# A reordered seam ahead of the first feed-forward: turning X before its row factors are known

## The reference

```python
o = jnp.concatenate([o_mla, o_gla], axis=-1) @ w_out[l]
x = x + gate_m * rms_norm(o, g_post_mix[l])

h = rms_norm(x, g_pre_ffn[l]) * (1.0 + scale_f) + shift_f
f = (jax.nn.silu(h @ w_ffn_gate[l]) * (h @ w_ffn_up[l])) @ w_ffn_down[l]
x = x + gate_f * rms_norm(f, g_post_ffn[l])
```

## Time and profile before

| | |
|---|---|
| median of 3 runs | 2699.1 us (2698.87 to 2699.74) |
| profiled execution, whole | 2705.51 us |
| its span | 2703.7 us |
| mean granted TensorE clock | 0.981 |

### The profile page before, as it was taken

The page is one execution under the profiler, slowest core; times in us unless marked ns, Lnnn a source line. Parts: engine busy times, 40 slices in busy tenths (PEclk is TensorE's granted clock), DMA queues, the critical chain, the costliest instruction groups (busy, mean ns, idle before and its releaser), DMA issues.

```text
span 2703.7 us, 30651 instructions
## 1 busy us (share of the span) xinstructions
PE 2602.7 (96%) x12149; PEld 2158.3 (80%) x12149; DVE 1668.6 (62%) x1700; ACT 1151.0 (43%) x1217; POOL 0.2 (0%) x4
## 2 busy tenths in 40 slices
PE   5899999899999999999999999999899999999998
PEld 4778778788887888887988888787688888888886
DVE  7878788856665555557446665655555555555556
ACT  5244544443333333335445455444653333333333
POOL 0000000000000000000000000000000000000000
PEclk8999999899999999999999999999999999999999
DMA  9979969977776555554854444554455555555553
GB/s 330 360 262 324 330 220 324 243 252 253 254 253 209 190 192 191 186 186 157 239 172 140 150 147 152 171 202 153 143 187 186 186 189 191 193 188 186 186 187 139
DMA packets 268139, 568.20 MB, mean 210 GB/s; under 512 B 9857, under 2 KB 46591, under 8 KB 258704
## 3 DMA queue, kind: packets, MB, share of 16 engines
q1 hardware_dynamic: 265986, 563.83, 61.9%
q10 hardware_dynamic: 2064, 3.15, 1.0%
HBM read 561.69 MB, written 5.24 MB: 210 GB/s over the span
## 4 chain that ended last, share of the span: by engine, by line
PE 80%; DVE 5%; ACT 3%; issue 2%; DMA 1%; DVEq 0%; ACTq 0%
PE bank L1283 25%; PE bank L1285 24%; PE bank L1284 24%; ACT wh L631 2%; DVE wl L1964 1%; DVE ROWB L1964 1%; DVE ACC L1985 1%; DMA raw<-in_w_out 1%; PE bank L1252 1%; PE bank L1816 1%; PE bank L1645 1%; PE bank L1764 1%; PE bank L1799 0%; DVE X L2118 0%; DMA raw<-in_w_uq 0%
## 5 line engine op out<-in xcount | busy, mean ns | idle before, releaser
L1964 DVE TENSOR_TENSOR wl<-raw,wh 128x2048 fp32r<-128x2048 f32 (+4 forms) x434 | 975.6, 2248 | 875.6 <-ACT wh L631 875.1
L631 ACT ACTIVATE wh<-raw 128x2048 fp32r<-128x2048 f32 (+4 forms) x434 | 816.4, 1881 | 1317.9 <-PE bank L1285 1209.8
L1283 PE MATMUL bank<-wh,XTh 128*128 128x512 f32 (+4 forms) x2680 | 1044.5, 390 | 21.9 <-DVE wl L1964 15.9
L1285 PE MATMUL bank<-wh,XTl 128*128 128x512 f32 (+4 forms) x2680 | 1032.5, 385 | 0.0
L1284 PE MATMUL bank<-wl,XTh 128*128 128x512 f32 (+4 forms) x2680 | 1031.6, 385 | 0.0
L1283 PEld LDWEIGHTS bank<-wh,XTh 128*128 128x128 f32 x2680 | 506.1, 189 | 126.8 <-issue 18.3
L1285 PEld LDWEIGHTS bank<-wh,XTl 128*128 128x128 f32 x2680 | 505.5, 189 | 94.4
L1284 PEld LDWEIGHTS bank<-wl,XTh 128*128 128x128 f32 x2680 | 506.2, 189 | 91.1 <-issue 0.5
L1283 PE MATMUL bank<-wh,HTh 128*128 128x512 f32 x640 | 251.1, 392 | 3.0 <-DVE ROWB L1964 3.0
L1285 PE MATMUL bank<-wh,HTl 128*128 128x512 f32 x640 | 249.2, 389 | 0.0
L1284 PE MATMUL bank<-wl,HTh 128*128 128x512 f32 x640 | 249.1, 389 | 0.0
(11 more groups left out here) (317 smaller groups left out, 1502.8 us busy)
## 6 DMA issues: line engine op xcount, KB each, us to landing
raw<-in_w_ada SPq DMA_DIRECT2D x96, 1024.0 KB, 6.3
raw<-in_w_in SPq DMA_DIRECT2D x48, 1024.0 KB, 5.2
raw<-in_w_ffn_gate SPq DMA_DIRECT2D x44, 1024.0 KB, 5.2
raw<-in_w_ffn_up SPq DMA_DIRECT2D x44, 1024.0 KB, 5.2
raw<-in_w_ffn_down SPq DMA_DIRECT2D x44, 1024.0 KB, 5.0
raw<-in_w_gate SPq DMA_DIRECT2D x44, 1024.0 KB, 5.2
raw<-in_w_up SPq DMA_DIRECT2D x44, 1024.0 KB, 5.1
raw<-in_w_down SPq DMA_DIRECT2D x44, 1024.0 KB, 5.0
```

The lines of the kernel that those rows point to most:

```text
L631: act.activation(wh[:, st.lin % 2, 0:width], raw[:, st.raw % 4, 0:width], ACT.Copy).then_inc(hi_made, 1)
L1283: pe.matmul(out_, hi_t[:, k, rows], w[0][:, q, :], start=first and q == 0, stop=False)
L1285: mm = pe.matmul(out_, lo_t[:, k, rows], w[0][:, q, :], start=False, stop=last and q == n - 1)
L1964: return dve.tensor_tensor(out_, a, b, op)
```

## The change

X is turned as it is, without the factor 1/rms of its rows, as soon as the pieces of X are added. The row factors, which lie one to a partition, have to be laid along the free dimension to be applied behind the turn: VectorE puts them on a diagonal (`DIAG` = identity times factor), TensorE multiplies a matrix of ones by it, and ScalarE copies the result to `WIDE_INV`. VectorE multiplies the turned groups by it on their way from PSUM to `FTMP`. Groups 0 and 1 go row block by row block, so that the first gate slab can start with row block 0; gain and shift are applied there by VectorE, and for groups 2 to 7 by ScalarE, which writes the high part and the float32 value with one activation each. `slab_mm` gets a hook `row_ready`. ScalarE's `hi()` for gate slab 1 goes ahead of the squares, which become four of 1024 columns; `chunk_left("o")` and the issue of the write of `rel_scratch` go behind the high parts of row block 1. Cut to its core:

```diff
...
-TURNS = [("mem", 8, 2), ("x", 8, 1), ("cq", 2, 2), ("ckv", 1, 2), ("o", 8, 0), ("f1", 8, 1), ("z2", 8, 2),
+TURNS = [("mem", 8, 2), ("x", 8, 1), ("cq", 2, 2), ("ckv", 1, 2), ("o", 8, 0), ("f1", 10, 0), ("z2", 8, 2),
...
+        FTMP = at("FTMP", [P, 4, 512], zb + 4 * 4096)
+        DIAG = at("DIAG", [P, RB, P], zb + 4 * 10240)
+        WIDE_INV = at("WIDE_INV", [P, SEQ], zb + 4 * 10496)
...
-            chunk_left("o")
-            act.wait_ge(S("rel_row"), 2)
-            act.dma_start(rel_d, relrow[:, :].unsqueeze(1).broadcast_to([NH, P, REL_W])).then_inc(S("rel_out"), 16)
+            hi()
+
+            def f1_wide(r):
+
+                act.wait_ge(S("turned"), TURN0["f1"] + 3 * r + 3)
+                f(WIDE_INV[:, P * r:P * r + P], PB[2][:, P * r:P * r + P], ACT.Copy, "f_wide")
+
+            def f1_row_hi(r, b):
+
+                act.wait_ge(S("f_made"), 2 * r + b + 1)
+                rows = slice(P * r, P * r + P)
+                f(XTh[:, 2 * b:2 * b + 2, rows], FTMP[:, b, :].rearrange("p (t n) -> p t n", t=2)[:, :, rows], ACT.Copy, "turn_hi")
+
+            def f1_group_hi(b):
+
+                act.wait_ge(S("gained"), TURN_N["x"] + 3 + b)
+                for kt in (2 * b, 2 * b + 1):
+                    half = slice(SEQ * (kt % 2), SEQ * (kt % 2) + SEQ)
+                    src = FTMP[:, b % 4, half]
+                    kw = dict(scale=modA[:, 3, kt:kt + 1], bias=modA[:, 2, kt:kt + 1])
+                    act.activation(XTh[:, kt, :], src, ACT.Identity, **kw)
+                    ins = act.activation(src, src, ACT.Identity, **kw)
+                ins.then_inc(S("turn_hi"), 1)
 
             def ffn(k, pre, after, more, gain=None):
 
                 if k == 0:
                     j = NORMS.index(pre)
                     for r in range(RB):
-                        for c in range(4):
-                            act.wait_ge(S("x_added"), 4 * r + c + 1)
-                            if c + r:
-                                act.wait_ge(S("x_sq"), 4 * r + c)
-                            f(JUNK2[:, 512 * c:512 * c + 512], X[:, r, 512 * c:512 * c + 512], ACT.Square, "x_sq",
+                        for c in range(2):
+                            if (r, c) == (1, 1):
+                                f1_wide(0)
+                            act.wait_ge(S("x_added"), 4 * r + 2 * c + 2)
+                            if r:
+                                act.wait_ge(S("x_sq"), c + 1)
+                            f(JUNK2[:, 1024 * c:1024 * c + 1024], X[:, r, 1024 * c:1024 * c + 1024], ACT.Square, "x_sq",
                               accum_out=xsq[:, r, c:c + 1])
-                            if (r, c) in ((1, 0), (1, 3)):
-                                act.wait_ge(S("squared"), RB * j + r + (c == 3))
-                                part = slice(0, 1) if c == 0 else slice(1, 2)
-                                f(nstat[:, j, 1, part], nstat[:, j, 0, part], ACT.Sqrt, "row_rooted" if c == 0 else "rooted",
-                                  scale=1.0 / D, bias=eps[:, 0:1])
-                turn_hi(pre, XTh, gain=gain, between=hi)
+                        if r:
+                            f1_row_hi(0, 0)
+                        act.wait_ge(S("squared"), RB * j + r + 1)
+                        f(nstat[:, j, 1, r:r + 1], nstat[:, j, 0, r:r + 1], ACT.Sqrt, "rooted" if r else "row_rooted", scale=1.0 / D,
+                          bias=eps[:, 0:1])
+                    f1_row_hi(0, 1)
+                    f1_wide(1)
+                    f1_row_hi(1, 0)
+                    f1_row_hi(1, 1)
+                    chunk_left("o")
+                    act.wait_ge(S("rel_row"), 2)
+                    act.dma_start(rel_d, relrow[:, :].unsqueeze(1).broadcast_to([NH, P, REL_W])).then_inc(S("rel_out"), 16)
+                    act.wait_ge(S("mod_ready"), 10)
+                    for b in range(2, 8):
+                        f1_group_hi(b)
+                        if b in (3, 5):
+                            hi()
+                else:
+                    turn_hi(pre, XTh, gain=gain, between=hi)
...
-                    if name == "f1":
-                        pe.wait_ge(S("normed"), RB * 3 + 1 + b // 2 + 1)
...
-            def slab_mm(banks, kts, width, first, last, lhs=None, row_done=None, row_free=None):
+            def slab_mm(banks, kts, width, first, last, lhs=None, row_done=None, row_free=None, row_ready=None):
 
...
+                    if row_ready is not None:
+                        row_ready(r)
...
+            def f1_turn(b, rows=range(RB)):
+
+                for k in range(2):
+                    for r in rows:
+                        mm = pe.transpose(PB[4 + b % 4][:, SEQ * k + P * r:SEQ * k + P * r + P],
+                                          X[:, r, P * (2 * b + k):P * (2 * b + k) + P], ident)
+                return mm
+
+            def f1_rows(r):
+
+                pe.wait_ge(S("turn_free"), TURN0["f1"] + 2 * r + 2)
+
...
-                            rows = X if k else ROWB
-                            turn_into(pre, lambda r, q: rows[:, r, P * q:P * q + P],
-                                      lambda: None,
-                                      lambda s: slab_mm((0, 1), ALL[4 * s:4 * s + 4], 512, s == 0, s == 3), "xo" if k else None)
+                            first_slab = lambda s: slab_mm((0, 1), ALL[4 * s:4 * s + 4], 512, s == 0, s == 3,
+                                                           row_ready=f1_rows if k == 0 and s == 0 else None)
+                            if k:
+                                turn_into(pre, lambda r, q: X[:, r, P * q:P * q + P], lambda: None, first_slab, "xo")
+                                return
+                            for r, b in ((0, 0), (0, 1), (0, 2), (1, 0), (1, 1), (0, 3), (1, 2), (1, 3)):
+                                pe.wait_ge(S("x_added"), 4 * r + b // 2 + 1)
+                                if b == 3:
+                                    pe.wait_ge(S("mod_ready"), 10)
+                                f1_turn(b, (r,))
+                            for r in range(RB):
+                                pe.wait_ge(S("normed"), RB * 3 + r + 1)
+                                pe.matmul(PB[2][:, P * r:P * r + P], ones, DIAG[:, r, :], start=True, stop=True)\
+                                    .then_inc(S("turned"), 3)
+                            first_slab(0)
+                            f1_turn(4).then_inc(S("turned"), 1)
+                            f1_turn(5).then_inc(S("turned"), 1)
+                            pe.wait_ge(S("turn_free"), TURN0["f1"] + 6)
+                            first_slab(1)
+                            f1_turn(6).then_inc(S("turned"), 1)
+                            f1_turn(7).then_inc(S("turned"), 1)
+                            pe.wait_ge(S("turn_free"), TURN0["f1"] + 8)
+                            first_slab(2)
+                            pe.wait_ge(S("turn_free"), TURN0["f1"] + 10)
+                            first_slab(3)
                             return
...
+            def row_squared(r):
+
+                dve.wait_ge(S("x_sq"), 2 * r + 2)
+                dve.tensor_reduce(nstat[:, n, 0, r:r + 1], xsq[:, r, 0:2], AX.X, ALU.add).then_inc(S("squared"), 1)
+
+            def row_diag(r):
+
+                dve.wait_ge(S("rooted"), n + 1) if r else dve.wait_ge(S("row_rooted"), 1)
+                dve.reciprocal(nstat[:, n, 2, r:r + 1], nstat[:, n, 1, r:r + 1]).then_inc(S("rooted_inv" if r else "row_inv"), 1)
+                dve.wait_ge(S("rooted_inv"), n + 1) if r else dve.wait_ge(S("row_inv"), 1)
+                dve.tensor_scalar(DIAG[:, r, :], ident, nstat[:, n, 2, r:r + 1], None, ALU.mult).then_inc(S("normed"), 1)
+
+            def f1_row_scaled(r, b):
+
+                dve.wait_ge(S("f_wide"), r + 1)
+                rows = slice(P * r, P * r + P)
+                src, dst = (t.rearrange("p (t n) -> p t n", t=2)[:, :, rows] for t in (PB[4 + b][:, :], FTMP[:, b, :]))
+                tt(dst, src, WIDE_INV[:, rows].unsqueeze(1).broadcast_to([P, 2, P]), ALU.mult).then_inc(S("gained"), 1)
+
+            def f1_row_made(r, b):
+
+                dve.wait_ge(S("gained"), TURN_N["x"] + 2 * r + b + 1)
+                for k in range(2):
+                    kt = 2 * b + k
+                    part = FTMP[:, b, SEQ * k + P * r:SEQ * k + P * r + P]
+                    ins = dve.tensor_scalar(part, part, modA[:, 3, kt:kt + 1], modA[:, 2, kt:kt + 1], ALU.mult, ALU.add)
+                ins.then_inc(S("f_made"), 1)
+
+            def f1_row_lo(r, b):
+
+                dve.wait_ge(S("turn_hi"), HI0["f1"] + 2 * r + b + 1)
+                rows = slice(P * r, P * r + P)
+                tt(XTl[:, 2 * b:2 * b + 2, rows], FTMP[:, b, :].rearrange("p (t n) -> p t n", t=2)[:, :, rows],
+                   f32(XTh[:, 2 * b:2 * b + 2, rows]), ALU.subtract).then_inc(S("turn_free"), 1)
+
+            def f1_group_scaled(b):
+
+                if b >= 4:
```

(64 more changed lines are left out.)

## The result

The changed kernel takes 2708.78 us (median of 8 runs, 2706.37 to 2712.82), the kernel before 2700.31 us in the same comparison (8 runs, 2698.87 to 2709.19). The ratio is 1.0023 with a 95% interval of 1.0014 to 1.0032, that is +6.2 us, between 3.8 and 8.6: slower, as forecast, and by less than the +10.1 forecast. It is a loss of 0.2%, small, but clear of zero.

A forecast was written before the change was run, and what follows sets the result against it. TensorE, busy 96% of the span, was taken as the bound. A later start of the second w_ffn_up slab (+7.9 us) and the low clock (2.2) sum to +10.1 on 2699.1, giving 2709.2 us; range 2703.5 to 2714.5.

The forecast's parts named there:

- (1): ScalarE: hi() for the second gate slab goes ahead of the squares, 1.92 us, from 505.1 to 507.0.
- (2): ScalarE: eight squares of 512 columns become four of 1024, 1.06 us each.
- (4): TensorE: 16 unscaled turns right behind mod_sum(4), 0.23 us each, to 512.1; row 0's product with ones to 512.6.
- (5): Row 0's wide factor, scaling and parts on ScalarE and VectorE: first gate slab starts at 516.0, 5.5 us earlier.
- (6): Row 1 in the same way: high parts to 518.5, low parts to 518.9, nothing waits.
- (7): Groups 2 to 7: first w_ffn_up slab starts at 542.7 instead of 545.12, 2.4 us won, VectorE the limit.
- (8): rel_scratch write issued 13.05 us later; second w_ffn_up slab waits for its end, TensorE starts that slab +7.9 us.
- The term for the clock: TensorE at the second w_ffn_up slab, after waiting 10.4 us: half speed costs 1.6 to 2.9 us, taken as 2.2.
- No second wait follows: Third and fourth w_ffn_up slabs land about 2.8 us apart against 5.45 of matmuls each, so no further wait.
- Rival A: Loads and write alternate on each DMA engine; second w_ffn_up slab lands near 534; 2696.7, not slower; chance 0.12.

The follow-up runs named there:

- e1: Changed kernel with chunk_left and the issue of the rel_scratch write put back behind the roots of o, ahead of hi(): 0.9999 of the kernel before.
- e2: Kernel before with only the rel_scratch write issued later, at the first hi() between the high parts: 1.0027 of the kernel before, +7.3 us.
- e3: e1 without TensorE's wait for mod_ready ahead of the whole feed-forward: 0.9998 of the kernel before.
- e5: Changed kernel with the write issued later, between the loads of the second and third w_ffn_up slabs: 1.0013 of the kernel before, +3.5 us.
- e9: Changed kernel with the write in four DMAs, the first at the same place, others behind high parts of groups 3, 5 and 7: 1.0002 of the kernel before.
- e4: Changed kernel with the write cut into two DMAs of half rows at the same place: 2710.25 us in a single run.
- e6: e3 with four moves: hi() of gate slab 1, mod_fin(4), row 0's product with ones, first w_ffn_up slab's lo() ahead of the memsets: 0.9996 of the kernel before.
- e7: e6 with the rel_scratch write issued late, where the change puts it: 1.0010 of the kernel before, +2.7 us.
- e8: e6 with the second w_ffn_up slab's lo() moved ahead of four of the eight memsets and the memset of ACC: 0.9996 of the kernel before.

## Why the prediction was right, and where it was off

The direction and the mechanism were right: the loss is the wait for up1 behind a write issued late, and not the seam's own work. e1 takes it away and e2 brings it alone. The time lies in the range (2708.8 in 2703.5 to 2714.5), and the forecast of +10.1 was 4 us too high. That the forecast time of 2709.2 is met within half a microsecond is luck: it is 2699.1 and 10.1, while the kernel before came out at 2700.3 in the longer comparison and the change at +6.2 by the ratio. Within the +10.1, too, errors of both signs partly cancelled, as the steps show. By its steps, all times from the first add:

- (1) and (2) held: `hi()` took 1.89 us, a square of 1024 columns 1.06.
- (4) missed a wait. The turns took 3.68 us as forecast, but began 2.7 us behind `mod_sum`. The code had it in plain sight: TensorE waits for `mod_ready` ahead of the whole `ffn(0, "f1")`, a line that the diff leaves alone. With the kernel before it cost nothing, since the turns then waited for the scaled rows anyway. The product with ones ended at 8.6 instead of 7.1. e3 prices this wait at 1.9 us.
- (5) and (6): the first gate slab started at 12.25 instead of 10.5, and the write was issued at 14.85 instead of 13.05, nearly all of both (1.5 of 1.8) by the wait of (4).
- (7) was mis-sized: up0 at 40.1 instead of 37.2, no gain of 2.4 but a loss of 0.5. 1.8 of these 2.9 is the late start of (5); another 0.9 is the low clock, which lasted for nearly the whole of row 0 of the first slab (its matmuls follow one another in 0.43 us for 5.0 us, at a granted clock of 0.50 in 515:520, not for 3.1). The wait of 0.41 ahead of the fourth slab was not forecast either. The one of 0.69 ahead of up0 was, with 1.0: VectorE is the limit there, as forecast.
- (8) failed in one step, "what was issued behind it waited for its end". The rows that the prediction read, 528:538 and 539:544, step over the end of the hold, and the write was nearly over by then. The 6 packets of q1 in 538:539 (shown at e5) were the hint that the load doesn't wait for the write's end. In the changed kernel up1 was held 14.0 us and then shared packet for packet. It landed at 43.6 instead of 48.8. TensorE started it at 47.9, against 53.1 forecast and 45.2 before: +2.8 instead of +7.9.
- The term for the clock was near: 0.50 from 551 to 554.3, a cost of 1.7 us against 2.2. It came without the 10 us of waiting that the forecast had ahead of it: TensorE had stood still for 2.1 us only, and in e2, behind 3.5 us, the clock fell as well (0.66 in the mean of 554 to 558). In e5 it did not fall behind 2.15 us, so this term is not certain at such a standstill, and these runs don't show what decides it.
- "No second wait follows" failed too, and for the same reason: with packets shared, up2 came 8.3 us behind up1 and not 2.8, and TensorE waited 0.94 for it. 2.8 + 1.7 + 0.9 makes 5.4 of the 5.7 us. The late issue by (5) and (6) made this larger and the sharing of (8) smaller than forecast.

Rival A was half right. It describes the second stretch (883 to 883) and not the first one (506 to none). The Trainium skill (DMA: Bandwidth & Descriptors, Queues, rings and completion order), which has each DMA engine go round robin between the queue rows, agrees with this trace from 537 on and not in 528:536. Had the queues shared from the start, up1 would have landed in time; e9 and e1 show what that is worth.

What stays open: what the load is held by for 12 to 14 us. A count of packets is ruled out (e4). So is a write that merely runs beside the load: a piece issued behind the load doesn't hold it (e9). The write's end is ruled out too. A time and a number of bytes are not told apart, and neither is quite constant: 12 us with leads of 17 to 20, 14 with leads of 4 to 5, 12.7 with the smaller packets. A lead under 4 us and a write that moves at a much slower rate were not tried.

## What to carry to other kernels

When an edit moves a line that issues a transfer, work out who is queued behind it at the new place, even if nobody waits for the transfer itself. A bulk write that is harmless under one cover costs the next loads their slack when it is issued 15 us later. Cut into pieces of some 8 us it cost nothing measurable at the late place (the early place wasn't tried with pieces). And when a wait is removed, read the code for older waits that it had hidden: here an untouched one ahead of the whole stage took 1.9 us of the gain, and memsets that e6 moved from ahead of up0's low part to ahead of up1's took another 1.4.

## What the runs showed of the hardware

- A load on SyncE's queue that is issued behind a large write of ScalarE's queue moves no packet for some 13 to 14 us with the write 4 to 5 us ahead (changed kernel, e2, e4, e5, e7), and for 12 with the write 17 to 20 us ahead (before, e1, e3, e6, e8). Behind a piece of 8 us it is held for 4.4 us only (e9). After the hold the two queues alternate about one to one. A load issued 0.3 us ahead of the write isn't held (5.3 us to landing in e5); there the write starts 3.9 us after its issue.
- The write of 1536 B runs moves at 97 GB/s, 0.25 us a packet of an engine (changed kernel, 528:536), that of 768 B runs at 92, 0.13 us a packet (e4). Loads of 2 KB runs alone move at 360 GB/s in 539:544, the start included, and at 408 in 541:544. While both share, the loads get 1.78 MB in 15 us, 119 GB/s, beside the larger packets and 220 beside the smaller ones.
- Issuing a second write of 2048 packets right behind the first stopped ScalarE for 5.95 us (e4); a single issue took 0.66. In e9 the first three pieces took 0.31 to 0.35 us each to issue and the fourth 2.59.
